# Block products of a hybrid encoder step: the first pair's last low part by VectorE instead of by a transfer

## The reference

```
def _mlp(x, g, w_up, w_down):
    h = _rmsnorm(x, g)
    return jnp.square(jax.nn.relu(h @ w_up)) @ w_down
...
    x = x + _merge(conv_out, attn_out, gates, w_out)
    x = x + _mlp(x, g_mlp, w_up, w_down)
```

## Time and profile before

| | us |
|---|---|
| median of 3 runs | 940.68 |
| lowest, highest | 939.51, 941.32 |
| the profiled execution | 939.73 |
| its span in the trace | 938.0 |
| PE busy | 925.6 (99%) |
| VectorE busy | 654.8 (70%) |
| ScalarE busy | 587.7 (63%) |
| POOL busy | 229.9 (25%) |

### The profile page before, as it was taken

One profiled execution on the slowest core, in us unless ns is written; L12 is line 12 of the kernel. 1 busy time (PEld: TensorE's weight loads), 2 busy tenths in 40 slices (PEclk: granted clock), 3 DMA queues, 4 the chain that ended last, 5 costly groups with the idle time before them and its releaser, 6 DMA issues.

```text
span 938.0 us, 19495 instructions
## 1 busy us (share of the span) xinstructions
PE 925.6 (99%) x7329; PEld 905.5 (97%) x7329; DVE 654.8 (70%) x1181; ACT 587.7 (63%) x980; POOL 229.9 (25%) x200
## 2 busy tenths in 40 slices
PE   8999999999999999999999999999999999999997
PEld 8999999999999999999999999999999999999997
DVE  6579999999999999998563335873488258722233
ACT  6787887878787878776833445653465356523353
POOL 5311010101010110101243443223422431244440
PEclk9999999999999999999999999999999999999999
DMA  7777667675858484859232233386238534852202
GB/s 183 156 175 136 171 126 179 118 186 104 180 113 192 101 196 99 172 131 208 60 111 80 81 89 90 92 177 161 68 95 183 150 90 90 191 134 87 85 23 96
DMA packets 194716, 120.95 MB, mean 129 GB/s; under 512 B 36014, under 2 KB 181854, under 8 KB 194667
## 3 DMA queue, kind: packets, MB, share of 16 engines
q1 hardware_dynamic: 176666, 80.28, 31.7%
q0 software_dynamic: 12816, 37.23, 22.3%
q10 hardware_dynamic: 5184, 2.78, 1.1%
HBM read 75.97 MB, written 7.06 MB: 89 GB/s over the span
## 4 chain that ended last, share of the span: by engine, by line
PE 92%; DMA 3%; ACT 2%; DVE 1%; POOL 1%; issue 1%; ACTq 0%; DVEq 0%
PE dense L661 67%; PE z L983 6%; PE dense L983 4%; PE z L781 3%; PE dense L955 3%; DMA w_lo<-w_raw 2%; PE z L745 2%; PE z L815 2%; POOL w_lo L614 1%; PE z L661 1%; DMA x_tok<-in_x_sample_dram 1%; PE z L749 1%; PE dense L825 0%; ACT n L1090 0%; PE z L947 0%
## 5 line engine op out<-in xcount | busy, mean ns | idle before, releaser
L661 PE MATMUL dense<-r_hi,w_hi 128*128 128x272 f32 (+1 forms) x1008 | 210.6, 291 | 1.4 <-ACT r_hi L1118 0.7
L661 PE MATMUL dense<-r_lo,w_hi 128*128 128x272 f32 (+1 forms) x1008 | 209.6, 289 | 0.0
L661 PE MATMUL dense<-r_hi,w_lo 128*128 128x272 f32 (+1 forms) x1008 | 209.5, 289 | 0.0
L632 POOL TENSOR_TENSOR w_lo<-w_raw,w_hi 128x1024 fp32r<-128x1024 f32 x56 | 134.6, 2409 | 197.3 <-ACT w_hi L1072 197.3
L1562 DVE SCALAR_TENSOR_TENSOR acc<-conv_in,cw_cur,acc 128x574 f32<-128x574 f32 x232 | 172.8, 811 | 0.5
L661 PEld LDWEIGHTS dense<-r_hi,w_hi 128*128 128x128 f32 x1008 | 158.2, 188 | 1.9 <-issue 0.9
L661 PEld LDWEIGHTS dense<-r_lo,w_hi 128*128 128x128 f32 x1008 | 158.7, 188 | 0.6 <-DVE r_lo L1543 0.6
L661 PEld LDWEIGHTS dense<-r_hi,w_lo 128*128 128x128 f32 x1008 | 159.0, 188 | 0.0
L1072 ACT ACTIVATE w_hi<-w_raw 128x1024 fp32r<-128x1024 f32 x110 | 115.3, 1052 | 34.0 <-PE z L983 22.0
L609 POOL DMA_DIRECT2D w_lo<-w_raw x53 | 45.1, 851 | 361.2 <-ACT w_lo L1074 361.2
L661 PE MATMUL dense<-s_hi,w_hi 128*128 128x272 f32 x640 | 132.2, 288 | 0.0
(11 more groups left out here) (301 smaller groups left out, 1913.3 us busy)
## 6 DMA issues: line engine op xcount, KB each, us to landing
w_raw<-in_w_in_dram SPq DMA_DIRECT2D x54, 512.0 KB, 5.5
w_lo<-w_raw POOLq DMA_DIRECT2D x53, 512.0 KB, 5.1
w_raw<-in_w_up_dram SPq DMA_DIRECT2D x32, 512.0 KB, 4.2
w_raw<-in_w_down_dram SPq DMA_DIRECT2D x32, 512.0 KB, 3.9
w_lo<-w_raw POOLq DMA_DIRECT2D x36, 256.0 KB, 4.7
w_raw<-in_w_pw_dram SPq DMA_DIRECT2D x8, 512.0 KB, 4.0
w_raw<-in_w_out_dram SPq DMA_DIRECT2D x8, 512.0 KB, 3.9
x_tok<-in_x_prompt_dram SPq DMA_DIRECT2D x4, 512.0 KB, 6.3
```

Source lines behind the costliest of these rows:

```text
L632: pool.tensor_tensor(w_lo[:, n], w_raw[:, n], w_hi[:, n].bitcast(F32), ALU.subtract).then_inc(lo_post, 1)
L661: mm = nc.tensor.matmul(out[:, h, 0:half], w[:, wslot, k, :], m[:, k, c0 + h * half:c0 + (h + 1) * half], start=(k == 0 and n == 0), stop= ...
```

## The change

In pair 0 of each of the three rounds, A22's low part is no longer made by ScalarE's negated copy and a transfer, but by one VectorE subtraction, raw less high, right after the low part of T4. It signals on a semaphore of its own, `first_lo`. The waits for A22's low part (TensorE's, and SP's before the load of pair 2's second block) go to `first_lo` for these pairs. Pairs 1 to 3 are as they were, with counts that leave the first pairs out.

```
+        def by_dma(P_, name):
+            return name in BY_DMA and not (name == "A22" and P_ % PAIRS == 0)
+
+        def low_signal(P_, name):
+            return (first_lo if name == "A22" else wform_lo[MADE[name] - 1]), 1
+
+        def low_wait(P_, name):
+            if name == "A22":
+                rounds = P_ // PAIRS + 1
+                return (wform_lo[MADE[name] - 1], 16 * (P_ + 1 - rounds)) if P_ % PAIRS else (first_lo, rounds)
+            return wform_lo[MADE[name] - 1], (16 if name in BY_DMA else 1) * (P_ + 1)
...
         def low_made(engine, P_, name):
-            engine.wait_ge(wform_lo[MADE[name] - 1], (16 if name in BY_DMA else 1) * (P_ + 1))
+            engine.wait_ge(*low_wait(P_, name))
...
             def seven_low(P_):
-                for name in BY_DMA:
+                for name in [name for name in BY_DMA if by_dma(P_, name)]:
...
-                    if name in BY_DMA:
+                    if by_dma(P_, name):
                         mm = nc.scalar.activation(form_place(w_lo, name), raw_form(P_, name), ACT.Copy, scale=-1.0)
...
                     u_low(rr, m, "B22", b22)
                     u_low(rr, m, "T4", usum("T4"))
+                    if f == KC - 1:
+                        wsum_low(PAIRS * rr, "A22")
...
             def wsum_low(P_, name):
-                if name not in BY_DMA:
+                if not by_dma(P_, name):
                     dve.wait_ge(wform_hi, PRODUCTS * P_ + MADE[name])
-                    nc.vector.tensor_tensor(form_place(w_lo, name), wsum(name), form_place(w_hi, name).bitcast(F32), ALU.subtract).then_inc(wform_lo[MADE[name] - 1], 1)
+                    nc.vector.tensor_tensor(form_place(w_lo, name), raw_form(P_, name), form_place(w_hi, name).bitcast(F32), ALU.subtract).then_inc(*low_signal(P_, name))
```

More of the change, by code:

```diff
@@ L291, in build @@
         wform_hi, wform_lo = sem("wform_hi"), [sem(f"wform_lo{n}") for n in range(PRODUCTS)]
-        wsum_done = sem("wsum_done")
+        wsum_done, first_lo = sem("wsum_done"), sem("first_lo")
         usum_done, form_hi, form_ready = sem("usum_done"), sem("form_hi"), sem("form_ready")
```

## The result

| | before | changed | ratio |
|---|---|---|---|
| median | 940.52 (20 runs) | 942.88 (20 runs) | 1.0023, 95% interval 1.0016 to 1.0030 |
| profiled execution, span | 939.73, 938.0 | 944.12, 942.3 | |

The changed kernel is slower by 2.4 us. The forecast was 943.0, which is 2.3 above the median known then (940.7).

A forecast was written before the change was run, and what follows sets the result against it. TensorE, busy 99% of the span, was taken as the bound. Round terms of +0.56, +0.88 and +0.84 gave +2.3 us on the profiled 939.73, so 942.0, plus 0.95 to the median: 943.0, range 939.0 to 945.2.

The forecast's parts named there:

- A22's stall goes: At pair 0's last product each round, TensorE's wait for the transfer vanishes; VectorE's extra 0.69 us fits in 0.8 us slack.
- The issues meet: After pair 0's subtraction, SP's load of pair 2's second block goes 2.8 us earlier, together with POOL's transfer for pair 1's A11.
- The price of the meeting: The transfer for pair 1's A11, issued beside the load, takes 5.5 us in rounds 1 and 2, 6.2 in round 0.
- The sum: Later starts of pair 1's A11, +1.05, +0.88, +0.84 in rounds 0 to 2, less 0.49 in round 0: +2.3 us.
- The case of the earlier trace at 591.0: At round 0's start, a POOL low transfer and an SP load issued 0.1 us apart took 7.2 and 6.1 us.
- The stall at A22 of pair 1 in round 0: TensorE's wait at 624.50 disappears, since its transfer is issued 1.5 us earlier while TensorE comes 1.05 later: -0.49 us.
- The case in which the change does what it says: At pair 1's A11 the transfer lands in 3.3 to 4.0 us, no price: 937.3 to 937.8; chance 0.17.
- The deciding point: TensorE reaches pair 1's A11 3.7 us after its transfer's issue; a landing up to there loses nothing.
- The mild meeting: The transfer for pair 1's A11 lands in 4.4 to 5.0 us: 939.0 to 940.8; chance 0.21.
- The Trainium skill's formula: For transfer and load together, about 2.0 us plus bytes over 436 GB/s: 768 KB in after an estimated 3.8 us.

## Why the prediction was right

- *A22's stall goes, at no cost on VectorE.* Right in all three rounds; in round 1 x22 was done 0.9 us ahead of its use.
- *The issues meet.* POOL's transfer was put 6.84 after the round's first matmul (702.05 for a round that began at 695.21) and came 6.84 after it (704.05 for 697.21), and SP's load with it.
- *The price of the meeting.* 5.5 was taken for rounds 1 and 2, and 5.8 measured; 6.2 for round 0, and 5.6 measured. The sum took round 0's transfers to be the longer ones everywhere, and here it was the shortest of the three. The case of the earlier trace rows at 591.0 repeats at its own place (7.5 us in the changed kernel).
- *The sum.* From S4's last matmul to A11 of pair 1, rounds 0, 1, 2: 3.11, 2.59, 2.62 before, 3.59, 3.86, 3.81 after. So +0.48, +1.27, +1.19, for +1.05, +0.88, +0.84 forecast. The stall at A22 of pair 1 in round 0 went as said (-0.49). Together +2.45, for +2.28 forecast. Two smaller gaps of round 0, which the prediction doesn't count, went as well: at S3 of pair 1 (620.68 to 621.03 before) and at S3 of pair 2 (632.03 to 632.27), 0.5 together. So the waits cost about 2.0 net. From first to last matmul the block products are longer by 1.08, 1.22 and 1.18 us; that is 3.5, of which the stretch at half clock is 1.5, and 2.0 is left. The other 0.9 of the 4.3 between the two profiled spans stands ahead of the first changed instruction: the block products begin at 603.65 in one and at 602.73 in the other.
- *Beyond the forecast.* The stretch at half clock was in no term. In executions without it, told apart by their mean clock, the changed kernel is 1.5 us slower than the kernel before, with it 3.6, and the median of 2.4 lies between. So the median agrees better with the sum than the mechanisms alone would have made it, and in that the 943.0 has luck in it: the sum is too large for the first kind of execution, by 0.8, and lacks a term for the second.
- *The rivals.* The case in which the change does what it says was priced at 937.3 to 937.8. The kernel with the load held until S4 has that time, 937.7. The deciding point, a landing within 3.7 us, was right too: with 3.9 to 4.0 TensorE waits 0.2 us. The mild meeting (4.4 to 5.0 us) didn't come in the changed kernel. The Trainium skill's formula ("DMA: Bandwidth & Descriptors", Anatomy of one DMA), by which both transfers together would be in after an estimated 3.8 us, doesn't describe this: the two measured 4.5 and 5.8 us.

## What to carry to other kernels

When a step is made earlier, list everyone who waits for its signal, not only the engine that it was made early for: here the same signal frees a buffer, and the load that it frees lands on the one transfer that is next late. Look in the trace for the pair of transfers that will meet; here it stood at the start of each round, where nobody waits for it. One wait on the queue of the load, until a point 1.0 to 2.5 us later, turned a loss of 0.23% into a gain of 0.26%.

## What the runs showed of the hardware that was not expected

TensorE's granted clock fell from 2.4 to 1.2 GHz for about 3.2 us after a wait of 1.8 us in the profiled execution of the changed kernel, and by the mean clocks about half of its executions have such a stretch; with waits of 3.4 us the profiled execution has one after each. A stretch cost about 1.5 us, nearly as much as the wait ahead of it. With five matmuls without use in the wait no execution showed it. And a transfer of 256 KB within SBUF is slowed by a load of 512 KB far more when both are issued at once (5.8 us for 3.3) than when the load follows 1.0 us later (3.9): issued at once, the load's packets went ahead of all of the transfer's.
